# Index scores in pairs of heads between the v tiles, and the k and q norms two tiles at a time with ScalarE multiplying

## The chip, the cores and the metric

The kernel runs on one core of one Trainium2 chip. The metric is the device time of one execution in microseconds. The core has TensorE (matrix products, 1.2 or 2.4 GHz as granted), VectorE, ScalarE and GpSimd, each with its own instruction queue, and SyncE, whose queue here issues most of the DMAs. The queues meet only at semaphores.

## The reference, cut to what matters

One step of a hybrid decoder layer for a prompt of 1024 rows and eight sample rows with 8192 cached keys each. One input projection of the normalised rows gives q, k, v, two gates, the index queries qi, one index key ki, the index weights wi and the inputs of a convolution.

```python
q = _rms_norm(zq.reshape(B, T, N_HEADS, HEAD_DIM), q_g)
k = _rms_norm(zk.reshape(B, T, N_KV_HEADS, HEAD_DIM), k_g)
...
# _index_select: for each query the 256 keys of the highest score
s = jnp.einsum('thd,ld->thl', qi, ki).astype(jnp.float32) * (IDX_DIM ** -0.5)
score = jnp.einsum('th,thl->tl', wi.astype(jnp.float32) * (N_IDX_HEADS ** -0.5), jax.nn.relu(s))
score = jnp.where(k_pos[None, :] <= q_pos[:, None], score, -jnp.inf)
_, idx = lax.top_k(score, k_sel)
```

Eight heads of 64 values, 8 index heads of 64, all in float32. The chosen keys are attended (the kernel masks the others), the convolution branch (31 taps a channel, layer norm, silu) runs beside it, both are gated, projected by w_out and added to x.

## The kernel before, in words

The order on every engine is written out by hand; PsumPlan hands out the eight PSUM banks b0 to b7 and makes each new user of a bank wait until the one before has been read. A projection whose rows lie on partitions is done in nine tiles (`natural(g, t)`, t = 8 the eight sample rows: eight products of 512 columns), one whose channels lie there in twelve pieces (`transposed(g, m)`: eight products of 344 columns). In the trace every float32 product is two MATMUL rows.

The stages of TensorE are: x transposed; kw (index keys and weights); glub and glua in pieces; qi in pieces; the index stage; v in tiles, ga and gc in pieces, beside the search; k and q in tiles with their norms and transpositions; the attention of the prompt by blocks of 128 queries, from the last block to the first, with the samples' attention in between; the output projection.

VectorE works through `taps`: 4 channel groups of 31 multiply-adds over 1024 columns (ctmp, L1267). Ahead of the last twelve of them it prepares Qb and Wb, the samples' index queries and weights, and the samples' own score (`sn`, L1294 to L1298). TensorE's `own_score()` (one small product of sn and selnew) stands behind the tenth of the twelve qi pieces and waits for it.

In the index stage, blocks i = 2 to 7 of queries have eight heads each over (i + 1) x 128 keys (blocks 0 and 1 keep all their keys). Per head ScalarE copies the queries into one half of qz, whose other half is zero (L1043); TensorE multiplies the whole height of 128 by kiT into a pair of banks, SA or SB; ScalarE takes the relu (L1058), and VectorE adds it with its weight into SC (L1310, L1313). Every five heads a turn of the cached keys comes between, eight in all: GpSimd gathers index keys into cin, VectorE transposes four tiles to ct (L1241), TensorE multiplies by Qb (`cached(n)`), ScalarE takes the relu to drelu, TensorE weighs it (`weigh`, drelu and Wb), ScalarE writes sc16a or sc16b, SyncE's DMAs bring it by way of memory to SD.

The search finds the 256th highest score of each row bit by bit in 32 rounds. VectorE writes candidates (candn, L1373) and counts three of the seven groups of rows, ScalarE the other four (sgj, L1088); between its rounds ScalarE evacuates v, ga and gc from PSUM, about one tile or piece a round. At its end stand the exact threshold and a scan (dC, L1406). Only then do the norms begin.

The norm stage goes through NORMED: k tiles 0 to 7, k of the samples, q tiles 7 to 0, q of the samples, numbered n = 0 to 17. TensorE computes tile n and transposes tile n - 3 (`norm_transpose`). ScalarE squares tile n to nsq (L1133) and copies the transposed tile to kT or qT. VectorE's `norm(n)` sums the squares of each head (L1482), takes the reciprocal root in a chain of twelve short instructions that each wait for the one before, multiplies the tile by it (L1493) and by the gain (L1497). zN has two places. Between the norms VectorE has masks for the six searched blocks (n = 2 to 7), positions of the chosen cached keys (n = 2 to 5, with TensorE's rank rows at n = 5 to 8), pages and addresses (n = 6, 7), the bias of those keys (n = 8, eight times L1469 and a sum) and the centring of the convolution (n = 9). ScalarE squares the centred halves (lnsq) and TensorE sums them in `row_variances`.

## Time and profile before

| | |
|---|---|
| median of 3 runs | 1040.39 us (1034.81 to 1040.89) |
| the profiled execution | 1040.58 us |
| its span from first to last instruction | 1038.8 us |
| mean granted clock of TensorE | 0.946 of 2.4 GHz |
| busy: TensorE, VectorE, ScalarE, GpSimd | 930.8, 694.0, 372.5, 85.4 us |
| chain that ended last: TensorE, VectorE, ScalarE | 72%, 21%, 3% of the span |

The times of the views are microseconds from the first instruction of the span. A busy share says how much an engine worked, not whether the end hung on it: that is to be read stage by stage, from what each engine waited for.

### The profile page before, as it was taken

Reading aid. Unit: us, or ns where it says so; the run is one execution under the profiler, and the core shown is the slowest. Engines: PE = TensorE matmul, PEld = TensorE weight load, DVE = VectorE, ACT = ScalarE, POOL = GpSimd, SP = SyncE. Lnnn points to the kernel's source line nnn. Section 1 sums busy time; section 2 is a strip of 40 time slices with the busy share of each in tenths; the row PEclk is TensorE's granted clock in tenths of the full one; section 3 lists DMA queues with packets and bytes.
Section 4 is the critical chain, followed back from the end, with each engine's and each line's share of the span. In section 5 each row is a group of like instructions: output and inputs, shape, how many; then the busy total and the mean of one; then the engine's idle time right before and its main releaser. Section 6 shows DMA issues by size and latency. Waiting matters only on the chain.

```text
span 1038.8 us, 11317 instructions
## 1 busy us (share of the span) xinstructions
PE 930.8 (90%) x3900; PEld 514.4 (50%) x3900; DVE 694.0 (67%) x1598; ACT 372.5 (36%) x830; POOL 85.4 (8%) x90
## 2 busy tenths in 40 slices
PE   3999999936899999999998899697598789999998
PEld 2866666713243444666643334353366555445432
DVE  5309987999896765888878889966487565432111
ACT  6310101102666656889700000122765364221000
POOL 0211010000541000000000000001011101310000
PEclk9999999877999999999999899788699789999999
DMA  8363020200662302001030000005012102320211
GB/s 291 108 188 62 1 81 3 83 0 1 203 210 83 112 34 84 26 22 61 0 102 21 21 20 12 0 1 210 21 52 61 31 11 62 104 100 31 71 62 42
DMA packets 35314, 69.82 MB, mean 67 GB/s; under 512 B 9609, under 2 KB 11953, under 8 KB 35249
## 3 DMA queue, kind: packets, MB, share of 16 engines
q1 hardware_dynamic: 28089, 43.93, 13.0%
q0 software_dynamic: 7168, 25.17, 7.4%
q8 instruction: 31, 0.51, 0.2%
q14 instruction: 26, 0.21, 0.1%
HBM read 58.46 MB, written 11.11 MB: 67 GB/s over the span
## 4 chain that ended last, share of the span: by engine, by line
PE 72%; DVE 21%; ACT 3%; issue 3%; DMA 1%; SPq 1%; DVEq 0%; ACTq 0%
PE ps L491 67%; DVE ctmp L1267 8%; PE ps L494 4%; DVE ct L1241 1%; DMA xn<-in_x_prompt 1%; DVE pv L1469 1%; ACT PTs L942 1%; ACT uT L1120 1%; DVE LB L1470 1%; DVE mcum L1395 0%; DVE zN L1493 0%; ACT relu L1058 0%; DVE pv L1435 0%; DVE uT L1675 0%; ACT sqj L955 0%
## 5 line engine op out<-in xcount | busy, mean ns | idle before, releaser
L491 PE MATMUL ps<-xT,W 128*128 128x344 f32 x960 | 283.8, 458 | 0.0
L491 PEld LDWEIGHTS ps<-xT,W 128*128 128x128 f32 x960 | 184.0, 193 | 97.6 <-issue 5.6
L491 PE MATMUL ps<-W,xT 128*128 128x512 f32 (+3 forms) x576 | 214.7, 531 | 1.2 <-ACT relu L1058 1.2
L1267 DVE SCALAR_TENSOR_TENSOR ctmp<-uT,chw,ctmp 128x1024 f32<-128x1024 f32 x116 | 152.0, 1310 | 4.1
L491 PEld LDWEIGHTS ps<-W,xT 128*128 128x128 f32 (+1 forms) x576 | 94.9, 185 | 113.7 <-issue 113.3
L1088 ACT ACTIVATE sgj<-SC,candn 128x1024 bf16<-128x1024 f32 (+3 forms) x128 | 114.5, 897 | 8.8 <-DVE candn L1373 6.6
L942 ACT ACTIVATE PTs<-ps 128x512 f32<-128x512 f32 (+3 forms) x96 | 43.1, 484 | 125.7 <-PE ps L494 125.7
L1706 DVE TENSOR_TENSOR ps<-ps,TP 128x256 f32<-128x256 f32 (+1 forms) x64 | 26.4, 412 | 71.2 <-PE ps L491 70.8
L1133 ACT ACTIVATE nsq<-ps 128x512 f32<-128x512 f32 (+1 forms) x18 | 10.7, 596 | 164.5 <-DVE nss L1482 120.9
L491 PE MATMUL ps<-kiT,qz 128*128 128x512 f32 (+3 forms) x160 | 61.7, 530 | 7.6 <-ACT relu L1058 6.5
L494 PE MATMUL ps<-Cc,Pm 128*128 128x128 f32 x288 | 46.6, 303 | 17.7 <-ACT PTs L942 17.5
L491 PE MATMUL ps<-W,uT 128*128 128x512 f32 x128 | 60.1, 612 | 0.0
L491 PE MATMUL ps<-W,qT 128*128 128x512 f32 x128 | 58.7, 600 | 0.0
L1711 DVE CUSTOM_DVE_ANT_0 Pm<-ps,SC 128x1024 f32<-128x1024 f32 (+7 forms) x64 | 48.5, 758 | 9.7 <-PE ps L494 7.7
L1785 POOL DMA_INDIRECT KVr<-in_cache_k,idx x16 | 16.0, 999 | 472.9 <-DVE zq L1497 369.8
L494 PEld LDWEIGHTS ps<-Cc,Pm 128*128 128x128 f32 x288 | 34.5, 153 | 40.1 <-issue 38.2
L1147 ACT ACTIVATE Pm<-Pm,mn 128x1024 f32<-128x1024 f32 (+7 forms) x64 | 49.5, 774 | 11.8 <-DVE mn L1711 11.2
L1686 DVE TENSOR_TENSOR resid<-resid,ps 128x512 f32<-128x512 f32 (+1 forms) x18 | 12.3, 684 | 60.8 <-PE ps L491 60.8
L1752 POOL DMA_INDIRECT cin<-in_cache_k_idx,pidx x32 | 36.8, 1149 | 170.3 <-DVE ct L1241 134.4
L491 PE MATMUL ps<-kT,qT 64*128 64x512 f32 (+3 forms) x192 | 44.6, 572 | 6.1 <-DVE mn L1711 3.6
L491 PEld LDWEIGHTS ps<-kiT,qz 128*128 128x128 f32 x160 | 27.8, 189 | 42.8 <-issue 39.0
L1313 DVE SCALAR_TENSOR_TENSOR SC<-relu,wI,SC 128x384 f32<-128x384 f32 (+5 forms) x42 | 39.7, 946 | 8.2 <-ACT relu L1058 6.1
(308 smaller groups left out, 1046.4 us busy)
## 6 DMA issues: line engine op xcount, KB each, us to landing
W<-in_w_in SPq DMA_DIRECT2D x8, 2048.0 KB, 8.7
xn<-in_x_prompt SPq DMA_DIRECT2D x8, 512.0 KB, 8.2
W<-in_w_out SPq DMA_DIRECT2D x1, 4096.0 KB, 13.3
resid<-in_x_prompt SPq DMA_DIRECT2D x16, 256.0 KB
out<-resid SPq DMA_DIRECT2D x16, 256.0 KB
out<-V SPq DMA_DIRECT2D x8, 256.0 KB
out<-zN SPq DMA_DIRECT2D x8, 256.0 KB, 2.0
bias_rows<-tprow SPq DMA_DIRECT2D x1, 1536.0 KB
```

Source lines behind the costliest of these rows:

```text
L491: return nc.tensor.matmul(out, lhsT, rhs, start=start, stop=stop)
L494: return nc.tensor.transpose(out, in_, ident[0:n, 0:n])
L942: nc.scalar.activation(out, in_, func, scale=scale).then_inc(plan.drain_sem(tag), 1)
L1088: last = nc.scalar.activation(sgj[:, j, 0:s.shape[1]], s, ACT.Sign, bias=candn[:, j:j + 1].bitcast(F32), accum_out=acnt[:, j:j + 1])
L1147: nc.scalar.activation(Pm[:, n % 3, 0:L], Pm[:, n % 3, 0:L], ACT.Exp, bias=mn[:, n % 4:n % 4 + 1], scale=-1.0, accum_out=sums[:, n:n + 1]) ...
L1267: ins = vec.scalar_tensor_tensor(conv[:, c, :] if j == CW - 1 else acc_, src, chw[:, c, j:j + 1], acc_, ALU.mult, ALU.add)
L1313: vec.scalar_tensor_tensor(sc(i), relu[:, n % 2, 0:L], wI[:, i, h:h + 1], sc(i), ALU.mult, ALU.add).then_inc(relu_used, 1)
L1686: vec.tensor_tensor(resid[u % 2][0:r, :], resid[u % 2][0:r, :], pt(("y", u))[0:r, :], ALU.add).then_inc(plan.drain_sem(("y", u)), 1)
L1706: link(vec.tensor_tensor(s[:, L - bw:L], s[:, L - bw:L], TP[:, h, BAND - bw:BAND], ALU.subtract))
L1711: vec.tensor_tensor_reduce(out=Pm[:, n % 3, 0:L], in0=s, in1=m, scale=1.0, scalar=3.0e38, op0=ALU.add, op1=ALU.min, accum_out=mn[:, n % 4: ...
L1752: pool.indirect_dma_start(out=cin[:, ch % 4, :], out_offset=None, in_=pages_ap, in_offset=bass.IndirectOffsetOnAxis(ap=pidx[:, ch % 8, ch ...
L1785: pool.indirect_dma_start(out=dst, out_offset=None, in_=src.rearrange("a n k h d -> (a n k) (h d)"), in_offset=bass.IndirectOffsetOnAxis(a ...
```

## The change

There are two edits. The first concerns the index stage. qz goes: a chunk is now a block, a pair of heads and at most 512 keys (CHUNKS, 40 of them), and TensorE multiplies the two heads from the two halves of qiT's height by the two halves of kiT's into two banks (b2 and b3, or b4 and b5). The chunks are spread over the slots of the v tiles: in each slot half of them stand in the middle of a v tile, and the others behind it (`halves`), the last block's eight in the ninth slot. v uses only b0 and b1. Relu has four places of 512 columns, where TP lies later, so that TP is loaded after the last weighting. sc16b lies in SC's last block, so that block waits until its DMAs are out (scd_out). ScalarE evacuates all nine v tiles in these slots, and the search starts with ga. VectorE does all its taps ahead of Qb, Wb and the own score, and TensorE's own_score() stands behind the second v tile. `cached_turn` 1 to 7 stand one to a slot, `cached` 0 to 5 likewise, and 6 and 7 together in slot 7.

The second edit concerns the norms. VectorE's chain runs for two tiles at once, at odd n; ScalarE multiplies (`scaled`, eight activations a tile, each with its own scale); VectorE multiplies by the gain only for k and the sample's q (`gained`), while q's gain goes into the scale with which qT is copied (qgc, loaded and scaled at the start). Transpositions and copies stand one tile later, and so do or two tiles later the other pieces between the norms; rank rows on TensorE stay.

```diff
-    relu = sb("relu", [P, 2, 1024], F32, rV)
-    sc16 = [sb("sc16a", [16, 32, 2, 16], F32, rKV), sb("sc16b", [16, 32, 2, 16], F32, rV + 8192)]
+    relu = sb("relu", [P, 4, 512], F32, rTP)
+    sc16 = [sb("sc16a", [16, 32, 2, 16], F32, rKV), sb("sc16b", [16, 32, 2, 16], F32, rSC + 12800)]
...
-    INDEX_STEPS = [(i, h) for i in range(2, NT) for h in range(H)]
+    CHUNKS = [(i, hp, a) for i in range(2, NT) for hp in range(H // 2) for a in range(0, (i + 1) * P, 512)]
+    def width(n):
+        i, hp, a = CHUNKS[n]
+        return min(512, (i + 1) * P - a)
+    FIRST_SLOT, SLOTS = 2, NT + 1
+    def chunks_in(s):
+        last = sum(1 for x in CHUNKS if x[0] < NT - 1)
+        if s == SLOTS - 1:
+            return range(last, len(CHUNKS))
+        k, n = s - FIRST_SLOT, SLOTS - 1 - FIRST_SLOT
+        return range(max(k, 0) * last // n, max(k + 1, 0) * last // n)
+    def cached_in(s):
+        return [6, 7] if s == 7 else [s - 1] if 1 <= s < 7 else []
+    def halves(s):
+        c = chunks_in(s)
+        return c[:len(c) // 2], c[len(c) // 2:]
+    EVACUATED_EARLY = NT + 1
...
-        def natural(g, t):
+        def natural(g, t, banks=4, between=None):
...
-            o = begin(("z", g, t), f"b{ring[0] % 4}")
+            o = begin(("z", g, t), f"b{ring[0] % banks}")
             ring[0] += 1
             for k in range(KC):
+                if between and k == KC // 2:
+                    between()
...
-                last.then_inc(ct_used, 1)
-            nc.tensor.matmul(ps[0:1, 6, 0:1], ident[0:1, 0:1], ident[0:1, 0:1], start=True, stop=True) \
-                .then_inc(plan.fill_sem(("ds", n)), 1)
+                last.then_inc(ct_used if g < 3 else plan.fill_sem(("ds", n)), 1)
...
-        done = 0
-        for n, (i, h) in enumerate(INDEX_STEPS):
-            wait(qz_ready, n + 1)
-            begin(("ix", i, h), ("SA", "SB")[n % 2])
-            L = (i + 1) * P
-            o = pair_of(("ix", i, h), L)
-            for a in range(0, L, 512):
-                b = min(a + 512, L)
-                last = mm(o[:, a:b], qz[:, h % 2, n // 2 % 2, :], kiT[:, a:b])
-            last.then_inc(plan.fill_sem(("ix", i, h)), 1)
-            while done < cached_before(n):
-                cached(done)
-                done += 1
-        for t in range(NT + 1):
-            natural("v", t)
+        def index_scores(n):
+            i, hp, a = CHUNKS[n]
+            for m in range(PIECES):
+                wait(*plan.drained(("zt", "qi", m)))
+            for t in range(i + 1):
+                wait(*plan.drained(("kt", t)))
+            for e in range(2):
+                begin(("ix", n, e), f"b{2 + 2 * (n % 2) + e}")
+            for e in range(2):
+                r = slice(64 * e, 64 * e + 64)
+                mm(pt(("ix", n, e))[:, 0:width(n)], qiT[r, hp, i * P:(i + 1) * P], kiT[r, a:a + width(n)]).then_inc(plan.fill_sem(("ix", n, e)), 1)
+        for s in range(SLOTS):
+            one, two = halves(s)
+            def between():
+                for n in one:
+                    index_scores(n)
+            natural("v", s, 2, between)
+            for n in two:
+                index_scores(n)
+            if s == 1:
+                own_score()
+            for n in cached_in(s):
+                cached(n)
...
-            wait(zn_ready, n + 1)
+            wait(zn_ready if g == "k" else z_scaled, n + 1)
...
-            if n >= 3:
-                norm_transpose(n - 3)
+            if n >= 4:
+                norm_transpose(n - 4)
...
+        def index_relu(n):
+            for e in range(2):
+                tag = ("ix", n, e)
+                u = 2 * n + e
+                act.wait_ge(*plan.full(tag))
+                if u >= 4:
+                    act.wait_ge(relu_used, u - 3)
+                nc.scalar.activation(relu[:, u % 4, 0:width(n)], pt(tag)[:, 0:width(n)], ACT.Relu, scale=HD ** -0.5).then_inc(plan.drain_sem(tag), 1)
...
+        for s in range(SLOTS):
+            for n in chunks_in(s):
+                index_relu(n)
+            for n in cached_in(s):
+                cached_out(n)
+            evacuate("v", s)
+        ev = EVACUATED_EARLY
...
-                     scale=1.0 if g == "k" else -HD ** -0.5)
+                     scale=1.0 if g == "k" else qgc[:, 0:1])
+        def scaled(n):
+            g, t = NORMED[n]
+            r = P if t < NT else NB
+            act.wait_ge(norms_ready, n // 2 + 1)
+            if n >= 2:
+                g2, t2 = NORMED[n - 2]
+                if t2 < NT:
+                    act.wait_ge(*plan.full(("tr", g2, t2)))
+                if g2 == "k":
+                    act.wait_ge(zn_out[n % 2], zn_stored(n - 2))
+            for h in range(H):
+                hs = slice(h * HD, (h + 1) * HD)
+                last = nc.scalar.activation(zN[0:r, n % 2, hs], pt(("z", g, t))[0:r, hs], ACT.Copy, scale=nrs[0:r, n % 2 * 8 + h:n % 2 * 8 + h + 1])
+            last.then_inc(plan.drain_sem(("z", g, t)), 1)
+            act.wait_ge(*plan.drained(("z", g, t)))
+            nc.scalar.activation(ss[0:NB, 15:16], ss[0:NB, 14:15], ACT.Copy).then_inc(z_scaled, 1)
...
-            if n >= 3:
-                norm_out(n - 3)
-            if n == 10:
+            if n >= 2 and n % 2 == 0:
+                scaled(n - 2)
+                scaled(n - 1)
+            if n >= 4:
+                norm_out(n - 4)
...
-        taps(CW + 24, NTAP - 12)
+        taps(CW + 24, NTAP)
...
+        def weighted(n):
+            i, hp, a = CHUNKS[n]
+            if (i, hp, a) == (NT - 1, 0, 0):
+                v.wait_ge(scd_out[1], 128)
+            for e in range(2):
+                u, h = 2 * n + e, 2 * hp + e
+                src, dst = relu[:, u % 4, 0:width(n)], sc(i)[:, a:a + width(n)]
+                v.wait_ge(*plan.drained(("ix", n, e)))
+                if h == 0:
+                    vec.tensor_scalar(dst, src, wI[:, i, 0:1], None, ALU.mult).then_inc(relu_used, 1)
+                else:
+                    v.wait_ge(relu_used, u)
+                    vec.scalar_tensor_tensor(dst, src, wI[:, i, h:h + 1], dst, ALU.mult, ALU.add).then_inc(relu_used, 1)
+        for s in range(SLOTS):
+            for n in chunks_in(s):
+                weighted(n)
+            if 1 <= s < 8:
+                cached_turn(s)
...
-            z = pt(("z", g, t))[0:r, :].rearrange("p (h d) -> p h d", h=H)
+            c = n % 2 * 8
             v.wait_ge(nsq_done, n + 1)
-            vec.reduce_sum(nss[0:r, :], nsq[0:r, :].rearrange("p (h d) -> p h d", h=H), AXX).then_inc(nsq_used, 1)
-            v.wait_ge(nsq_used, n + 1)
-            link(vec.tensor_scalar(nss[0:r, :], nss[0:r, :], 1.0 / HD, EPS, ALU.mult, ALU.add))
-            rsqrt(nrs[0:r, :], nss[0:r, :], ntm[0:r, :])
+            vec.reduce_sum(nss[0:r, c:c + 8], nsq[0:r, :].rearrange("p (h d) -> p h d", h=H), AXX).then_inc(nsq_used, 1)
+            if n % 2:
+                v.wait_ge(nsq_used, n + 1)
+                if n >= 3:
+                    v.wait_ge(z_scaled, n - 1)
+                link(vec.tensor_scalar(nss[:], nss[:], 1.0 / HD, EPS, ALU.mult, ALU.add))
+                rsqrt(nrs[:], nss[:], ntm[:])
+                vec.memset(dsc[:, 7:8], 0.0).then_inc(norms_ready, 1)
+        def gained(n):
+            g, t = NORMED[n]
+            if (g, t) != ("q", NT) and g == "q":
+                return
+            r = P if t < NT else NB
             o = zN[0:r, n % 2, :].rearrange("p (h d) -> p h d", h=H)
-            if n >= 2:
-                g2, t2 = NORMED[n - 2]
-                if t2 < NT:
-                    v.wait_ge(*plan.full(("tr", g2, t2)))
-                if g2 == "k":
-                    v.wait_ge(zn_out[n % 2], zn_stored(n - 2))
-            vec.tensor_tensor(o, z, nrs[0:r, :].unsqueeze(2).broadcast_to([r, H, HD]), ALU.mult).then_inc(plan.drain_sem(("z", g, t)), 1)
-            v.wait_ge(*plan.drained(("z", g, t)))
+            v.wait_ge(z_scaled, n + 1)
...
+            if n >= 3:
+                gained(n - 3)
...
+        for half in range(2):
+            sp.dma_start(qgc[64 * half:64 * half + 64, :], qg[0:1, :].rearrange("a d -> d a"), allow_slow_non_contiguous=True).then_inc(q_gain_in, 16)
...
+        sp.wait_ge(relu_used, 2 * len(CHUNKS))
+        sp.wait_ge(tp_out, 16)
+        sp.dma_start(TP[:], bass.AP(tpd.tensor, P - 1, [[FW - 1, P], [P * FW, H], [1, BAND]])).then_inc(tp_in, 16)
```

On TensorE, between the last qi pieces and the second cached turn, before (kiT with qz are the index scores, ct with Qb a cached turn, drelu with Wb its weighing):

```order
L491 MATMUL ps<-xT,W 128x344 x24
L491 MATMUL ps<-sn,selnew 128x1
L491 MATMUL ps<-xT,W 128x344 x16
L491 MATMUL ps<-kiT,qz 128x384 x5
L491 MATMUL ps<-ct,Qb 32x512 x8
L638 MATMUL ps<-Cc 1x1
L491 MATMUL ps<-kiT,qz 128x384 x3
L491 MATMUL ps<-kiT,qz 128x512 x2
```

and of the changed kernel (W with xT are eight or four products of a v tile, kiT with qiT the pairs):

```order
L516 MATMUL ps<-xT,W 128x344 x40
L516 MATMUL ps<-W,xT 128x512 x16
L516 MATMUL ps<-sn,selnew 128x1
L516 MATMUL ps<-ct,Qb 32x512 x8
L516 MATMUL ps<-W,xT 128x512 x4
L516 MATMUL ps<-kiT,qiT 128x384 x4
L516 MATMUL ps<-W,xT 128x512 x4
L516 MATMUL ps<-kiT,qiT 128x384 x4
L516 MATMUL ps<-kiT,qiT 128x512 x2
L516 MATMUL ps<-ct,Qb 32x512 x8
L516 MATMUL ps<-drelu,Wb 16x512
```

The own score moved behind the two qi pieces and two v tiles, the first cached turn right behind it, and each later v tile is cut in two by chunks.

On VectorE, from the third group of taps to the first index scores, before:

```order
L1267 SCALAR_TENSOR_TENSOR ctmp<-uT,chw,ctmp 128x1024 x18
L1280 COPY Qb<-ps 32x8x8 x4
L1286 MEMSET dsc 128x1
L1288 TENSOR_TENSOR Wb<-ps,Cc 128x4x4x4
L1294 TENSOR_TENSOR zN<-srow,kiS 8x512
...
L1298 TENSOR_REDUCE sn<-sn 8x1
L1300 TENSOR_TENSOR SD<-ps,Cc 128x1
L1267 SCALAR_TENSOR_TENSOR ctmp<-uT,chw,ctmp 128x1024 x11
L1267 SCALAR_TENSOR_TENSOR uT<-uT,chw,ctmp 128x1024
L1310 TENSOR_SCALAR SC<-relu,wI 128x384
L1313 SCALAR_TENSOR_TENSOR SC<-relu,wI,SC 128x384 x4
```

and of the changed kernel:

```order
L1317 SCALAR_TENSOR_TENSOR ctmp<-uT,chw,ctmp 128x1024 x29
L1317 SCALAR_TENSOR_TENSOR uT<-uT,chw,ctmp 128x1024
L1330 COPY Qb<-ps 32x8x8 x4
L1336 MEMSET dsc 128x1
L1338 TENSOR_TENSOR Wb<-ps,Cc 128x4x4x4
L1344 TENSOR_TENSOR zN<-srow,kiS 8x512
...
L1348 TENSOR_REDUCE sn<-sn 8x1
L1350 TENSOR_TENSOR SD<-ps,Cc 128x1
L1291 STREAM_TRANSPOSE ct<-cin 128x1024 x4
L1362 TENSOR_SCALAR SC<-relu,wI 128x384
L1365 SCALAR_TENSOR_TENSOR SC<-relu,wI,SC 128x384 x7
```

The last twelve taps stand ahead of Qb, Wb and sn, and a turn of transpositions ahead of the first weighting.

On ScalarE at the start of the norms, before (nsq are squares, kT the copy of a transposed tile):

```order
L1133 ACTIVATE nsq<-ps 128x512 x4
L942 ACTIVATE kT<-ps 128x4x128
L1133 ACTIVATE nsq<-ps 128x512
L942 ACTIVATE kT<-ps 128x4x128
L1133 ACTIVATE nsq<-ps 128x512
L942 ACTIVATE kT<-ps 128x4x128
L1133 ACTIVATE nsq<-ps 128x512
```

and of the changed kernel (zN from ps and nrs are the eight multiplications of a tile, ss the short copy behind which z_scaled is raised):

```order
L1174 ACTIVATE nsq<-ps 128x512 x3
L1147 ACTIVATE zN<-ps,nrs 128x64 x8
L1150 ACTIVATE ss<-ss 8x1
L1147 ACTIVATE zN<-ps,nrs 128x64 x8
L1150 ACTIVATE ss<-ss 8x1
L1174 ACTIVATE nsq<-ps 128x512 x2
L1147 ACTIVATE zN<-ps,nrs 128x64 x8
L1150 ACTIVATE ss<-ss 8x1
L1147 ACTIVATE zN<-ps,nrs 128x64 x8
L1150 ACTIVATE ss<-ss 8x1
L975 ACTIVATE kT<-ps 128x4x128
L1174 ACTIVATE nsq<-ps 128x512
```

Two tiles are multiplied at each even n, ahead of the copies, and the squares of the next tile stand behind the second of them.

## Rows read from the trace of the kernel before

**Rows 1.** Two stretches: busy time of each engine, clock, DMA share, GB/s

```profile
253.00:346.00 93.00, 84.77 (x320) 33.09 (x320) 76.59 (x78) 60.72 (x119) 30.56 (x31) 1.00 0.51 164
547.00:716.00 169.00, 148.01 (x453) 68.21 (x451) 137.81 (x389) 23.11 (x41) 0.00 (x0) 0.91 0.06 20
```

**Rows 2.** Timeline of TensorE, 239 to 520 us (start, duration, operation, count, idle before)

```profile
239.72 0.58 PE L491 MATMUL ps<-sn,selnew 8*128 8x1 f32 x2 [23.96 <-DVE sn L1298]
240.23 11.77 PE L491 MATMUL ps<-xT,W 128*128 128x344 f32 x32
258.09 1.94 PE L491 MATMUL ps<-ct,Qb 128*32 128x512 f32 x16
268.97 1.03 PE L491 MATMUL ps<-drelu,Wb 128*16 128x512 f32 x2
331.19 14.00 PE L491 MATMUL ps<-kiT,qz 128*128 128x512 f32 x32
346.40 62.13 PE L491 MATMUL ps<-W,xT 128*128 128x512 f32 x144 [1.21 <-ACT relu L1058]
408.46 111.31 PE L491 MATMUL ps<-xT,W 128*128 128x344 f32 x384
```

**Rows 3.** TensorE in the attention stage: pairs of 1024 and 512 columns

```profile
750.86 1.99 PE L491 MATMUL ps<-kT,qT 64*128 64x512 f32 x8
871.13 1.13 PE L491 MATMUL ps<-kT,qT 64*128 64x512 f32 x4
```

**Rows 4.** Timeline of VectorE: last taps, weightings, transpositions

```profile
240.41 14.49 DVE L1267 SCALAR_TENSOR_TENSOR ctmp<-uT,chw,ctmp 128x1024 f32<-128x1024 f32 x11
256.66 2.79 DVE L1313 SCALAR_TENSOR_TENSOR SC<-relu,wI,SC 128x384 f32<-128x384 f32 x4
260.11 4.62 DVE L1241 STREAM_TRANSPOSE ct<-cin 128x1024 f32<-128x1024 f32 x4 [0.66 <-PE ps L491]
346.29 1.28 DVE L1313 SCALAR_TENSOR_TENSOR SC<-relu,wI,SC 128x1024 f32<-128x1024 f32 x1 [0.43 <-ACT relu L1058]
```

**Rows 5.** VectorE in the search: candidates 1, 12 and 31, and dC

```profile
352.87 0.17 DVE L1373 TENSOR_SCALAR candn<-thr 128x4 uint32<-128x4 uint32 x1
423.64 0.17 DVE L1373 TENSOR_SCALAR candn<-thr 128x4 uint32<-128x4 uint32 x1
510.77 0.17 DVE L1373 TENSOR_SCALAR candn<-thr 128x4 uint32<-128x4 uint32 x1
533.96 1.23 DVE L1406 TENSOR_TENSOR_SCAN dC<-dE 128x513 f32<-128x513 f32 x1
```

**Rows 6.** Groups of ScalarE by form: count, busy us, mean ns, idle before

```profile
L1043 ACT ACTIVATE qz<-qiT 64x128 f32<-64x128 f32 x48 | 14.7, 307 | 1.2
L970 ACT ACTIVATE kiN<-ps 128x128 f32<-128x128 f32 x8 | 2.2, 278 | 11.2 <-PE ps L491 11.2
```

**Rows 7.** VectorE's norm of one tile, and the group of key bias products

```profile
550.30 0.66 DVE L1482 TENSOR_REDUCE nss<-nsq 128x8 f32<-128x512 f32 x1
553.41 0.69 DVE L1493 TENSOR_TENSOR zN<-ps,nrs 128x512 f32<-128x512 f32 x1
...
L1469 DVE TENSOR_TENSOR pv<-ohb,rbB 128x512 f32<-128x512 f32 x8 | 8.7, 1084 | 0.2
```

**Rows 8.** TensorE in the norm stage, and its first scores

```profile
550.68 8.81 PE L491 MATMUL ps<-W,xT 128*128 128x512 f32 x16
661.38 1.12 PE L494 MATMUL ps<-Cc,zN 128*128 128x128 f32 x4 [10.21 <-DVE zN L1497]
716.32 3.42 PE L491 MATMUL ps<-kT,qT 64*128 64x512 f32 x8 [2.49 <-DVE zN L1493]
```

**Rows 9.** SyncE's queue, and the landing times of the loads of W

```profile
331.96 2.62 SPq L1871 DMA_DIRECT2D decode_scores<-sc16b  x4
336.76 0.35 SPq L1874 DMA_DIRECT2D SD<-decode_scores  x1
...
DMA to landing us min/median/max: 8.0/8.9/12.0
```

116 lines of the change are left out of this document (42 added, 74 removed).

## The prediction

> **What bounds the kernel now.** I read the timeline of TensorE first, then that of VectorE for the stretches in which TensorE waits, then the table of windows. From 31 us on TensorE works almost without a gap; only four places matter here. (1) After ten of the twelve pieces of qi it waits 23.96 us for the sample's own index score, which VectorE reaches late among its taps [rows 2]. (2) From 253 to 346 us, the index stage, TensorE is busy 84.8 us of 93 and VectorE 76.6 us: the two hand each head to each other [rows 1]. (3) The search on VectorE and ScalarE runs from 348.2 to 535.2 us, and TensorE covers it with v (62.1 us), ga and gc and four k tiles; TensorE gets to the end of them only at 547 us, so in this stretch it is the bound [rows 2, 5]. (4) From 547 to 716 us come the k and q norms: TensorE busy 148.0 us of 169 and VectorE 137.8, with one wait of 10.21 us for VectorE and short ones besides [rows 1, 8]. What follows 716.32 us (322.5 us) holds the same instructions afterwards, and I carry it over unchanged.
>
> **Taps to own score.** The last 12 taps move ahead of the own score. At 1.32 us each (14.49/11, [rows 4]) they are 15.8 us, so the score, ready at 239.7 us before, is ready at 255.5. All of VectorE's work up to 256.2 us is the same work in another order, so VectorE starts on index scores when it did. TensorE gets two qi pieces at 4.64 us (111.31/24 for such pieces, [rows 2]) and two v tiles at 6.9 us ahead of the wait, which began at 215.8 us: 215.8 + 9.3 + 13.8 = 238.9 us, and then 16.6 us of wait instead of 24. So of the nine v tiles only two lie beside the taps: own_score stands behind the second one, and everything behind it waits. The idle time drops the granted clock; the two pieces after the old wait took 11.77 us instead of 9.3 [rows 2], so I charge 2.5 us for the way back to full clock, as before.
>
> **Index stage.** Seven v tiles, 40 chunks and eight turns of cached scores now stand in a row on TensorE. Prices: v tile 62.13/9 = 6.9 us; a cached turn 1.9 + 1.0 us for its weighing [rows 2]. A pair of heads on half the rows each: 1.99 us for 1024 columns and 1.13 us for 512 [rows 3], against 1.75 us for one head of 1024 before (14.00/8, [rows 2]). That is 1.67 ns a column for both heads, plus 0.2 us where the shape changes. All 40 chunks: 16,896 columns, 28.2 us, and 14 to 40 changes, 3 to 8 us: 31 to 36.5 us, I take 34 (26 of it ahead of the last eight chunks). It was 61.7 before, so pairing saves 28 us of TensorE. From 256.0 us: cached turn 1.9, six tiles 41.4, chunks 26, seven turns 13.3, eight weighings 7.7, clock 2.5 = 92.8 us, to 348.8. The seventh and eighth turn stand back to back, and the eighth needs four transposes (4.62 us, [rows 4]) that VectorE starts only when the seventh frees the tiles: 4 to 5 us of wait, to 353.
> VectorE is not the bound until then: a weighting costs 0.70 us at 384 columns and 1.32 at 1024 start to start [rows 4], so 0.33 us plus 0.97 ns a column; cutting at 512 adds 32 instructions, 10 us. Its sum is 43 us for the first 32 chunks and 32 for the transposes, 75 of 97 us; its slack sits in the half tiles of v that it waits for. The last eight chunks (block 7, all 512 wide) turn it round: 16 weightings at 0.82 = 13.1 us. They may start when the last decode scores have left sc16b. Before, their four DMAs began to be issued at 331.96 us and the DMA that waits for their landing at 336.76 [rows 9]: 4.8 us, so at 358.5; TensorE interposes half a tile (3.45 us) once, which costs about 1 us. VectorE ends at 373.1 instead of 347.6: **the stage costs 25.5 us more**. Bounds: 18 us if pairs and handovers are at their cheap end, 36 if each handover of a chunk shows as it did in the old stage, where VectorE idled 16 of 93 us [rows 1].
> W for ga is issued behind the scores' DMAs, at about 359 us, and needs 8.0 to 12.0 us to land [rows 9]: 367 to 371 us, and TensorE wants it at 368 to 369. Up to 2 us, in the slack ahead of the first evacuation. TP's load moves behind it; it is needed at 715 us and costs nothing. The two small loads of qgc put at most some 3 us before the page indices near 30 us, hidden since the gathered pages are first wanted at 48.5 us.
>
> **Search.** Rounds paced by v took 6.87 us; rounds with a piece or nothing take (510.77 - 423.64)/19 = 4.586 us [rows 5]. From the first candidate to the last it was 157.9 us for 30 rounds; now 30 x 4.586 + 0.7 for one table load = 138.3: **19.6 us less**. The head of it (4.7 us) and the 24.4 us from the last candidate to dC stay [rows 5]. The search starts at 373.8 (0.7 us for the mask on POOL) and dC stands at 541.2 instead of 535.2. TensorE runs out of work at about 508 us (111 us of ga and gc, 28 us of four k tiles) and idles 33 us: cover that v gave and that the search no longer needs.
>
> **Norms.** VectorE per tile now: a sum 0.7, and per two tiles one chain of 12 short steps (553.41 - 550.30 less the sum of 0.7: 2.4 us, [rows 7]). It loses 9 chains (22 us), 18 multiplications (0.72, 13 us) and the gain of eight q tiles (6 us): 41 us. ScalarE takes over eight activations of 64 columns a tile. The nearest rows: 128 columns from PSUM 278 ns, of which the next one overlaps 0.1 us, and from SBUF 307 ns [rows 6]. I take 8 x 0.13 + 0.1 + 0.2 for the closing copy = 1.4 us, bounds 1.0 and 2.7.
> The Trainium skill, "VectorE: DVE Perf Modes", section on the TRN2 errata, speaks against such narrow instructions: each pays its fixed part, 172 cycles on ScalarE from PSUM. As an estimate from that page eight of them are 1.6 us, which would add about 0.5 us at each of three handovers; the overlapping starts of rows 6 speak for less.
> Followed, with dC as zero (before in brackets): k4 starts at 8.8 (15.5), since the fifth tile needs only the first multiplied one; but the first transposition waits for VectorE behind a mask, and the rank rows are through at 35 (36). The key bias block (eight products of 1.1 and eight sums of 0.7 us, 14.6 us with the gaps, [rows 7]) moves two tiles on, beside q5, the two means and q4, so the 10.21 us wait [rows 8] goes: q4 starts at 101.5 (109). Three waits take its place. ScalarE in its order multiplies tile n-1 only when the transposition of n-3 has run, one tile later on TensorE, and the squares for the row variances stand behind that: 3.7 and 4.2 us. A new wait stands in each chain too: nrs is there once, so VectorE may overwrite it only when the pair before is multiplied; masks, position rows and with them TensorE's rank rows are queued behind. By hand it is met in time, at the closest by 1 us. At the end the last two tiles go one after the other through squares, chain, multiplication and copy: 6 us. Slow tiles behind waits and narrow products (8.81 against 6.9 us, [rows 8]) I counted as often as before. The scores start at 174.2 instead of 181.1: **6.9 us less**.
>
> **Sum.** 25.5 - 19.6 - 6.9 = -1.0. The profiled execution took 1040.58 us, 1.8 more than its span of 1038.8, and the median of the three is 1040.39. Forecast: 1040 us, no change. About 1% is what a measurement of this kernel can tell from none.
>
> **Rivals.** *The norms run at TensorE's own pace (faster).* TensorE's busy time from 547 to 716 is 148 us [rows 1]. If ScalarE is never late, the 14 us of the three waits go: 1026 us. For it: ScalarE is idle most of this stretch. Against: its order is fixed and has the later transposition in it. Chance 0.22.
> *The norms in twos hold TensorE (slower).* If VectorE, behind masks and position rows, finishes a chain late, or waits there for the pair before, the tile four further on finds no free bank, and TensorE waits once per pair: 2 us in seven pairs, 14 us: 1054 us. It decides where a pair's chain comes after two tile times (14 us). For it: VectorE is busy 137.8 of 169 us there today [rows 1]; against: 41 us leave it. Chance 0.2.
> *The edit doesn't do what it says:* the pairs do not overlap among full-height tiles, and TensorE pays up to 28 us in the stage that it bounds: 1066 us. Against it: the pairs of the attention stage do [rows 3]. Chance 0.08.
>
> **How the numbers follow.** Forecast 0.5. The range holds it, the first rival and the second with 3 us at the upper end for the index bounds: 1025 to 1057; outside are the third and the tails. Faster by over 1% 0.25, within 0.47, slower 0.28.
>
> **What would show it.** Wait before the own score about 17 us; last weighting near 373; candidates 4.6 us apart from the first; TensorE idle some 33 us before the end of the search; scores' start near 715. I am wrong if TensorE isn't busy through the v tiles after 256 us, if the rounds aren't short at once, or if the norm stage takes other than 165 to 185 us from dC to the scores.

## The result, and the profile after

The changed kernel takes 1064.56 us (median of 4, 1063.41 to 1067.55) against 1039.84 us before (median of 4): ratio 1.025, 95% interval 1.022 to 1.028. It is slower by 25 us. The forecast of 1040 us was wrong, and the range of 1025 to 1057 us did not hold the time. The profiled execution took 1065.68 us with a span of 1063.9 us, its mean granted clock of TensorE was 0.919 (0.946 before). Three of the twelve executions of one kernel below, the index edit alone, and single ones of five others took 12 us or more longer at a lower clock; the medians below leave these out, so that 1041.8 us stands where some expectations say 1042.7.

Four marks divide both traces; the difference of the last column is what the forecast has to answer for.

| | before | after | difference | forecast |
|---|---|---|---|---|
| search starts | 348.2 | 379.9 | +31.7 | +25.5 |
| search start to dC | 187.0 | 167.2 | -19.8 | -19.6 |
| dC to first scores | 181.1 | 192.6 | +11.5 | -6.9 |
| first scores to end of span | 322.5 | 324.2 | +1.7 | 0 |

The marks of after, first VectorE's, then TensorE's (timeline: start, duration, line, operation, count, idle before and what ended it):

```profile
379.91 0.06 DVE L1418 MEMSET candn<- 128x4 uint32 x1 [0.46 <-POOL SC L1841]
...
545.92 1.23 DVE L1459 TENSOR_TENSOR_SCAN dC<-dE 128x513 f32<-128x513 f32 x1
```

```profile
256.32 0.58 PE L516 MATMUL ps<-sn,selnew 8*128 8x1 f32 x2 [18.23 <-DVE sn L1348]
257.20 3.67 PE L516 MATMUL ps<-ct,Qb 128*32 128x512 f32 x16 [0.30 <-issue]
...
547.20 0.59 PE L516 MATMUL ps<-dC,Cc 128*128 128x1 f32 x2 [32.93 <-DVE dC L1459]
...
669.74 0.60 PE L519 MATMUL ps<-Cc,zN 128*128 128x128 f32 x4
674.55 6.99 PE L516 MATMUL ps<-Cc,lnsq 128*128 128x1 f32 x32 [4.21 <-ACT lnsq L1155]
681.39 10.15 PE L516 MATMUL ps<-W,xT 128*128 128x512 f32 x16
...
704.07 6.54 PE L516 MATMUL ps<-Cc,lnsq 128*128 128x1 f32 x32 [4.77 <-ACT lnsq L1155]
710.46 9.28 PE L516 MATMUL ps<-W,xT 128*128 128x512 f32 x16
...
738.72 1.09 PE L519 MATMUL ps<-Cc,zN 128*128 128x128 f32 x4 [6.53 <-ACT qT L975]
739.73 1.23 PE L516 MATMUL ps<-kT,qT 64*128 64x512 f32 x2
```

The reader is to see three things. The wait for the own score is 18.2 us where it was 24.0 [rows 2]. TensorE now idles 32.9 us ahead of dC, where before it came to dC 12 us late. And the tiles behind the row variances that had to wait are slow: 10.15 and 9.28 us, while an undisturbed one takes 7.0.

The table of windows of after (length, busy time of TensorE, of its loads, VectorE, ScalarE, POOL, granted clock), to be laid beside [rows 1]; the last line is the norm stage:

```profile
257.00:359.30 102.30, 95.27 (x368) 34.49 (x369) 70.69 (x93) 40.28 (x93) 27.96 (x31) 0.98 0.39 126
380.00:547.00 167.00, 134.28 (x434) 82.03 (x432) 147.88 (x571) 127.53 (x289) 0.00 (x0) 0.91 0.13 45
547.00:740.00 193.00, 159.87 (x454) 76.77 (x456) 108.59 (x281) 56.02 (x204) 0.00 (x0) 0.84 0.13 48
```

VectorE is relieved (108.6 us of 193, against 137.8 of 169 in [rows 1]; from dC to the scores its busy time fell from 142.2 to 108.4 us, by 34 where the forecast, which counts the gaps within its chains too, had 41), and it buys nothing: the clock fell from 0.91 to 0.84 and TensorE waits 33 us in all.

### The profile page after: what moved, and what is told of

It is laid out like the page before. It is cut to its first block, busy times and chain, and to the rows that moved or that the text cites. A ratio compares the mean times of both kernels' runs of the same rounds, so it can differ in the third digit from the quotient of the medians.

```text
span 1063.9 us, 11407 instructions
## 1 busy us (share of the span) xinstructions
PE 920.2 (86%) x3884; PEld 508.4 (48%) x3884; DVE 667.1 (63%) x1506; ACT 389.5 (37%) x976; POOL 82.3 (8%) x89
## 4 chain that ended last, share of the span: by engine, by line
PE 58%; DVE 21%; ACT 16%; issue 3%; DMA 1%; SPq 0%; DVEq 0%; ACTq 0%; POOL 0%; POOLq 0%
PE ps L516 54%; ACT sgj L1110 11%; DVE ctmp L1317 8%; PE ps L519 4%; DVE SC L1365 1%; ACT zN L1147 1%; DMA xn<-in_x_prompt 1%; ACT PTs L975 1%; DVE eqm L1386 1%; ACT uT L1161 1%; DVE mcum L1448 1%; DVE thr L1430 1%; DVE tk L1429 1%; DVE candn L1426 1%; DVE cnt L1404 1%
## 5 line engine op out<-in xcount | busy, mean ns | idle before, releaser
L516 PE MATMUL ps<-xT,W 128*128 128x344 f32 x960 | 280.8, 455 | 0.3 <-ACT relu L1079 0.3
L516 PE MATMUL ps<-W,xT 128*128 128x512 f32 (+3 forms) x576 | 221.9, 541 | 4.4 <-ACT zN L1147 4.4
L516 PEld LDWEIGHTS ps<-W,xT 128*128 128x128 f32 (+1 forms) x576 | 95.7, 188 | 123.2 <-issue 118.1
L1365 DVE SCALAR_TENSOR_TENSOR SC<-relu,wI,SC 128x512 f32<-128x512 f32 (+3 forms) x70 | 46.2, 660 | 25.1 <-ACT relu L1079 18.8
L1079 ACT ACTIVATE relu<-ps 128x512 f32<-128x512 f32 (+3 forms) x80 | 36.2, 526 | 51.7 <-PE ps L516 51.5
L1147 ACT ACTIVATE zN<-ps,nrs 128x64 f32<-128x64 f32 (+1 forms) x144 | 31.2, 322 | 55.9 <-PE ps L519 32.3
L1813 POOL DMA_INDIRECT cin<-in_cache_k_idx,pidx x32 | 33.1, 1034 | 198.8 <-DVE ct L1291 161.8
```

Of the source, the lines that this page charges most:

```text
L516: return nc.tensor.matmul(out, lhsT, rhs, start=start, stop=stop)
L1079: nc.scalar.activation(relu[:, u % 4, 0:width(n)], pt(tag)[:, 0:width(n)], ACT.Relu, scale=HD ** -0.5).then_inc(plan.drain_sem(tag), 1)
L1147: last = nc.scalar.activation(zN[0:r, n % 2, hs], pt(("z", g, t))[0:r, hs], ACT.Copy, scale=nrs[0:r, n % 2 * 8 + h:n % 2 * 8 + h + 1])
L1365: vec.scalar_tensor_tensor(dst, src, wI[:, i, h:h + 1], dst, ALU.mult, ALU.add).then_inc(relu_used, 1)
L1813: pool.indirect_dma_start(out=cin[:, ch % 4, :], out_offset=None, in_=pages_ap, in_offset=bass.IndirectOffsetOnAxis(ap=pidx[:, ch % 8, ch ...
```

## The experiments

All kernels are built on one of two: the changed kernel, or the index edit alone. Each was timed in five rounds beside the kernel before; times are medians, ratios are against the kernel before. Stages are read from one traced execution of each kernel, which need not be the median one. The start of the index stage drifts by some 2 us between kernels with the same code up to there (the own score at 255.1 to 257.5 us), so a stage's end is read from the own score.

**The two edits apart.** The first takes every line of the diff that belongs to the v tiles and the index scores, the second every line of the norms. In the norm stage the two differ in this:

```
-                norm_transpose(n - 3)
+                norm_transpose(n - 4)
...
+            if n >= 2 and n % 2 == 0:
+                scaled(n - 2)
+                scaled(n - 1)
```

> The index edit alone, with the norms of the kernel before. If the two edits act each in its own stage and do not touch each other, this takes the 31.7 us that the index stage lost and the 19.8 us that the search gave back, and keeps the norm stage of before at 181 us from dC to the first scores: about 1052 us (1050 to 1055). If the norm stage is slow in the changed kernel because of what the index edit did ahead of it (33 us in which TensorE idles before dC, where before it idled 23), the norm stage takes about 190 us here too and the kernel about 1062 us.

> The norms edit alone, with the index stage of the kernel before. If the norms in twos are themselves what costs, dC to the first scores takes 190 to 194 us instead of 181 and the kernel 1050 to 1053 us. If the cost came from the index edit ahead of it, this is at or below 1040 us, down to 1033 us if the forecast of 174 us for the norm stage holds.

Index edit alone: 1041.8 us, ratio 1.002 (1.000 to 1.005). Norms alone: 1062.6 us, 1.022 (1.019 to 1.025). So the norms edit carries 22 us of the 25. The index edit came out 10 us below the 1052 us expected, nearly all of it the head start told below. It is no matter of what stands ahead of it: dC to the scores took 171.9 us in the first (545.8 to 717.7), 20.7 less than in the changed kernel, and 201.9 us in the second (537.3 to 739.2), 20.8 more than before (this trace, of 1068.3 us, is the slowest of the six executions). The expectation for the norms alone was too low (190 to 194 us): the comparison with before had hidden that the index edit by itself makes this stage 9.2 us shorter (171.9 against 181.1), because TensorE stands ready at dC with its four k tiles done and not 12 us behind it. Windows of the norm stage, index edit alone, then norms alone:

```profile
546.00:718.00 172.00, 149.57 (x454) 69.92 (x456) 142.50 (x405) 24.21 (x43) 0.00 (x0) 0.89 0.10 37
```

```profile
537.00:739.00 202.00, 170.11 (x481) 81.61 (x479) 108.83 (x281) 56.04 (x203) 0.00 (x0) 0.87 0.12 45
```

Between the first and the changed kernel TensorE runs the same 454 instructions. It is idle 22.4 us in the one and 33.1 us in the other, and busy 149.6 against 159.9: half of the 20.7 us are waits, half are slower products.

**The clock, by products that nobody reads.** In the changed kernel:

```
+        def fill(count, bank):
+            for _ in range(count):
+                mm(ps[:, bank, :], xT[:, 0, 0:P], xT[:, 0, 0:512])
...
+            fill(36, 7)
             wait(made["equals_counted"], 1)
```

> The changed kernel with products that nobody reads (xT times xT, 512 columns) put on TensorE where it waited: 36 ahead of the first use of dC, 4 and 5 behind that, 4 and 5 ahead of the two row variances, 7 ahead of the last but one transposition. They are meant to end just before the wait does. Theory: the norm stage loses to the granted clock, which was 0.84 of full speed in it, and tiles of 7.0 us took 8.7 to 10.2 us right behind the waits; with the gaps filled the clock stays up, the tiles take 7.0 us, and dC to the scores falls by 10 to 14 us to 179 to 183 us, the kernel to 1050 to 1055 us. Rival: the waits on ScalarE and the coupling by twos are the cost, and the clock only a sign of them: then nothing is gained, 1064 to 1067 us.

1056.4 us, ratio 1.015 (1.012 to 1.018): 8.2 us less, of which 6.2 between dC and the scores (186.4 us) and 3.0 behind them. The clock up to dC was 1.00 instead of 0.91, and the first tile behind dC took 7.03 us instead of 9.46. The time lies between what the theory (1050 to 1055 us) and its rival (1064 to 1067 us) expected. The tiles that cost most stayed slow:

```profile
668.90 3.60 PE L516 MATMUL ps<-xT 128*128 128x512 f32 x8
673.27 5.67 PE L516 MATMUL ps<-Cc,lnsq 128*128 128x1 f32 x32 [0.78 <-ACT lnsq L1171]
678.80 10.18 PE L516 MATMUL ps<-W,xT 128*128 128x512 f32 x16
...
701.51 3.73 PE L516 MATMUL ps<-Cc,lnsq 128*128 128x1 f32 x32 [0.49 <-ACT lnsq L1171]
705.10 8.81 PE L516 MATMUL ps<-W,xT 128*128 128x512 f32 x16
```

The tile behind the row variances took 10.18 and 8.81 us with no long wait ahead. So a slow tile needs no long wait ahead of it: in the index edit alone the tile behind the second row variances (32 products of one column, with no wait) takes 8.81 us too. The clock is part of the loss, and the 10 to 14 us expected of it were too many.

**The squares ahead of the scaling.** ScalarE's order in the changed kernel, two lines moved:

```
+            if n == 12:
+                squares(0, half_of(0), lnsq)
...
             if n >= 2 and n % 2 == 0:
                 scaled(n - 2)
                 scaled(n - 1)
...
-            if n == 12:
-                squares(0, half_of(0), lnsq)
```

> The changed kernel with ScalarE squaring the centred halves ahead of the two tiles that it scales, where it now does it behind them. Both waits of TensorE ahead of its row variances (4.2 and 4.8 us) should go. If the waits themselves are the cost, 9 us less: 1055 us. If the clock is, each wait removed also spares the slow tile behind it (3.1 and 2.3 us): 1050 us. If the products then wait for the scaled tiles instead (their banks come free 3 us later), 1062 to 1065 us.

1051.8 us, ratio 1.011 (1.008 to 1.013), 12.8 us less, near the 1050 us expected if each wait also costs a slow tile; dC to the scores 179.4 us. Of the two waits one is left with 1.9 us:

```profile
670.41 6.66 PE L516 MATMUL ps<-Cc,lnsq 128*128 128x1 f32 x32 [1.91 <-ACT lnsq L1155]
676.93 9.15 PE L516 MATMUL ps<-W,xT 128*128 128x512 f32 x16
...
693.66 3.63 PE L516 MATMUL ps<-Cc,lnsq 128*128 128x1 f32 x32
697.15 8.81 PE L516 MATMUL ps<-W,xT 128*128 128x512 f32 x16
```

7.1 us of waiting went, and with it 4.7 us in the products behind: the second row variances run in 3.63 us instead of 6.54, the other three in 6.66, 9.15 and 8.81 instead of 6.99, 10.15 and 9.28. This one order is over half of what the norms edit lost.

**The tail too.** On top of the run before, separate columns of nss, nrs and ntm for alternate pairs, and ScalarE takes the square of the last tile ahead of `scaled(15)`.

```
-                if n >= 3:
-                    v.wait_ge(z_scaled, n - 1)
+                if n >= 5:
+                    v.wait_ge(z_scaled, n - 3)
...
+            if n == 17:
+                scaled(15)
+                norm_out(12)
+                norm_out(13)
```

> The changed kernel with the squares first, as in the run before it that took 1051.8 us, and with its tail mended: two sets of columns for the norms, so that the last pair's reciprocal roots start without waiting for the pair before, the square of the last tile ahead of the fifteenth tile's scaling. If the 8 us that TensorE waits in the tail are the chain of ScalarE and VectorE work behind the last tile, 3 to 5 us go: 1047 to 1049 us, and the norms in twos then cost 4 to 6 us against the index edit alone at 1042.7 us. If the chain only shifts to another wait, 1051 to 1052 us.

1051.6 us, ratio 1.010 (1.007 to 1.014): level with the run before, where 1047 to 1049 us had been hoped for. The scores start earlier (175.8 us behind dC), but take longer, 327.6 us against 324.7. TensorE's waits between dC and the scores are now 23.0 us in all, as good as the 22.4 of the index edit alone. The first 40 us of the scores in three kernels, index edit alone, the changed one, this one:

```profile
717.70:757.70 40.00, 26.37 (x156) 15.43 (x156) 26.39 (x37) 26.50 (x40) 5.04 (x6) 0.83 0.29 110
```

```profile
739.70:779.70 40.00, 26.93 (x123) 15.19 (x124) 22.61 (x34) 26.35 (x38) 5.02 (x5) 0.71 0.12 35
```

```profile
721.60:761.60 40.00, 27.39 (x109) 15.29 (x108) 21.03 (x32) 24.78 (x36) 5.02 (x5) 0.59 0.19 69
```

The clocks of 0.83, 0.71 and 0.59 go with 320.8, 324.2 and 327.6 us from the first scores to the end. The same work is done more slowly: 4.9 of the 6.8 us between the first and the last of the three lie in the first 54 us. That the handovers of the tail are the reason is not shown. The kernel before has the same tail as the index edit alone, and its first 40 us run at 0.71.

**Scaling on ScalarE without the twos.** The changed kernel, with each tile's norm by itself and the squares at n = 10 and 13 as before; position rows, pages and key biases stand one tile later than before.

```
-            if n >= 2 and n % 2 == 0:
-                scaled(n - 2)
-                scaled(n - 1)
-            if n >= 4:
-                norm_out(n - 4)
+            if n >= 1:
+                scaled(n - 1)
+            if n >= 3:
+                norm_out(n - 3)
```

> The changed kernel with ScalarE still multiplying and the gains of q still in the transposition's copy, but each tile's norm by itself again, transposed three tiles later and not four, the row variances' squares where they were before. This parts the two halves of the norms edit. If the twos cost the 20.7 us (each tile waits for its partner, ScalarE's two scaled tiles in a row stand ahead of the squares), it takes 1038 to 1043 us, like the index edit alone. If ScalarE's scaling in eight pieces is the cost, even one at a time, 1050 to 1060 us.

1052.0 us, ratio 1.014 (1.011 to 1.017), within what the second theory expected, which put the cost on ScalarE's scaling even one tile at a time. From dC to the scores it takes 181.8 us, 9.9 more than with the norms of before and 10.8 less than the changed kernel, so the first theory keeps a part. The first transposition now waits 10.0 us where two waits of 4.7 and 1.8 stood, since a k tile passes from VectorE to ScalarE and back to VectorE for its gain; the transposition ahead of the row variances waits for ScalarE:

```profile
559.06 1.12 PE L519 MATMUL ps<-Cc,zN 128*128 128x128 f32 x4 [10.01 <-DVE zN L1552]
...
680.97 1.11 PE L519 MATMUL ps<-Cc,zN 128*128 128x128 f32 x4 [6.61 <-ACT ss L1150]
```

So the scaling on ScalarE costs some 10 us in this form. The other 10.8 us can't be put down to the pairing as such: with the twos kept and only the squares first, the stage took 179.4 us, 2.4 less than with the tiles one at a time. What the twos cost in the changed kernel is above all the place of the squares behind two scaled tiles.

**Filling in two more kernels.** First the kernel with both repairs, filled like the first but not ahead of the row variances (36, 4, 5, and 5 ahead of the last transposition but one); then the index edit alone, filled with 36, 5, 2 and 10:

```
+            if n == 3:
+                fill(5, 7)
+            if n == 12:
+                wait(*plan.drained(("tr",) + NORMED[6]))
+                fill(10, 4)
             if n >= 3:
                 norm_transpose(n - 3)
```

> The changed kernel with both repairs of its norm stage (1051.6 us), and filling products: 36 ahead of the first use of dC, 4 and 5 behind it, 5 ahead of the last transposition but one. The first 40 us of the scores, which ran at a granted clock of 0.50 and 0.65 behind the waits of the tail (0.80 and 0.84 with the norms of before), should run at 0.8, worth 4 to 6 us there, and the first tile behind dC at full clock, worth 2 us: 1043 to 1047 us. If the low clock in the scores has another reason than the waits ahead of them, 1049 to 1051 us.

> The index edit alone, norms of before, with products that nobody reads where TensorE waits: 36 ahead of the first use of dC (it waits 32.9 us there), 5 and 2 between the first normed tile and the second use of dC (4.7 and 1.8 us), 10 ahead of the tenth tile's transposition (9.1 us). Three tiles behind those waits took 9.6, 8.8 and 9.1 us where others took 7.0. If the clock is what they lose, 5 to 7 us go: 1036 to 1038 us against 1042.7 us without them. If the filling ends too late or the clock is lost elsewhere as before (the rank rows, the row variances), 1041 to 1044 us.

The repaired one fell from 1051.6 to 1043.4 us, 1.006 (1.003 to 1.008). All of that lies behind the first scores (318.2 us instead of 327.6); dC to the scores stayed at 175.2. The time is the one expected, the way to it only in part: of the 9.4 us only 3.4 lie in the first 54 us of the scores, whose first 40 us ran at 0.74 and not 0.8, and why the rest went is open. The index edit alone rose from 1041.8 to 1051.0 us, 1.009 (1.006 to 1.013), against both theories. Up to the two means it keeps pace (95.6 us behind dC, 95.0 without filling); then, in the filled kernel and in the one without:

```profile
656.23 8.75 PE L511 MATMUL ps<-xT 128*128 128x512 f32 x20
666.66 0.66 PE L514 MATMUL ps<-Cc,zN 128*128 128x128 f32 x4 [1.68 <-DVE zN L1532]
...
675.78 0.66 PE L514 MATMUL ps<-Cc,zN 128*128 128x128 f32 x4 [1.59 <-DVE zN L1532]
676.27 6.33 PE L511 MATMUL ps<-Cc,lnsq 128*128 128x1 f32 x32
682.46 9.39 PE L511 MATMUL ps<-W,xT 128*128 128x512 f32 x16
```

```profile
663.85 1.12 PE L514 MATMUL ps<-Cc,zN 128*128 128x128 f32 x4 [9.11 <-DVE zN L1519]
664.76 9.05 PE L511 MATMUL ps<-W,xT 128*128 128x512 f32 x16
673.65 0.60 PE L514 MATMUL ps<-Cc,zN 128*128 128x128 f32 x4
674.09 3.63 PE L511 MATMUL ps<-Cc,lnsq 128*128 128x1 f32 x32
677.58 7.11 PE L511 MATMUL ps<-W,xT 128*128 128x512 f32 x16
```

Filling the 9.1 us wait moved the low clock from one tile (9.05 us) to the row variances and the next tile (6.33 and 9.39 instead of 3.63 and 7.11), and the scores behind it run slower (325.6 us against 320.8). Its single times lie between 1040 and 1052.5 us, wider than without filling (1040 to 1047 us), so where the low stretch falls may also change from one execution to the next; a single trace can't show that. Why it falls where it does is open; that a filled wait always pays is refuted.

**The key biases spread.** Index edit alone, three, three and two heads in three tiles, the centring and the first half's squares one tile later.

```
-            if n == 8:
-                for h in range(H):
+            if 8 <= n <= 10:
+                for h in range(3 * (n - 8), min(3 * (n - 7), H)):
                     key_bias(h)
-            if n == 9:
+            if n == 10:
                 center(0, 0, half_of(conv, 0), 512)
```

> The index edit alone, norms of before, with the eight key biases (14.7 us of VectorE work in one piece, behind which TensorE waits 9.1 us for a normed tile and then runs at low clock) spread over three tiles, and the centring one tile later. If that piece is what TensorE waits for, the wait and the slow tile behind it go, 5 to 10 us: 1033 to 1038 us. If VectorE is simply full there (busy from 605 us to 672 us without a break), the wait comes back in pieces: 1041 to 1043 us.

1046.1 us, ratio 1.007 (1.004 to 1.010): slower by 4.3 us than without, and outside both expectations. The wait of 9.1 us shrank to 2.7, but the squares came later, and TensorE waited 7.45 us for them at the row variances, with 6.98 us for those. As in the changed kernel, squares that come late are paid for at the row variances.

**What holds the end of the index stage.** Index edit alone, `sc16b` in the taps' region instead of the last block's; then the last block's chunks spread over all slots and the eighth cached turn in the last slot:

```
-sb("sc16b", [16, 32, 2, 16], F32, rSC + 12800)
+sb("sc16b", [16, 32, 2, 16], F32, rGC)
...
-        last = sum(1 for x in CHUNKS if x[0] < NT - 1)
-        if s == SLOTS - 1:
-            return range(last, len(CHUNKS))
-        k, n = s - FIRST_SLOT, SLOTS - 1 - FIRST_SLOT
+        last = len(CHUNKS)
+        k, n = s - FIRST_SLOT, SLOTS - FIRST_SLOT
```

> The index edit alone, with the second buffer of the cached scores in a place of its own, so that VectorE no longer waits 10.6 us for its transfer ahead of the last block; the last block's chunks stay in the last slot. Theory: TensorE sets the end of the index stage and brings the last block's products no earlier than 361.5 us, so VectorE gets at most 1 us: 1041.5 to 1043 us. Rival: the transfer was what held the stage, and 5 to 8 us go: 1035 to 1038 us.

> As the run before, and the last block's chunks spread over all seven slots instead of the last one, with the eighth cached turn in the last slot instead of behind the seventh. TensorE's work is the same, but its three waits around the last two turns (1.8 and 1.5 us, and some 2 us of low clock) are covered and VectorE no longer runs 4 us behind TensorE at the end. Theory: 5 to 9 us less in the index stage, 1034 to 1038 us. Rival: the decode scores, whose transfer to SD takes 10 us from the last turn, now end the stage, and what is gained is 0 to 3 us: 1040 to 1043 us.

1041.5 us, 1.002 (0.999 to 1.004), as the theory said, and 1045.0 us, 1.004 (1.001 to 1.006), slower than theory and rival. From the own score to the search: 123.2 us for the index edit alone, 123.6, and 120.9. The wait for the transfer turned into one for the products, as the theory had it:

```profile
365.29 0.49 DVE L1331 TENSOR_SCALAR SC<-relu,wI 128x512 f32<-128x512 f32 x1 [9.62 <-ACT relu L1076]
```

The spreading gained 2.3 us there against the index edit alone, within the rival's 0 to 3, and the search took 170.5 instead of 167.2 us. TensorE stood without weights at its start:

```profile
376.42 8.94 PE L509 MATMUL ps<-xT,W 128*128 128x344 f32 x22 [3.98 <-DMA W<-in_w_in]
```

**The load earlier, and v tiles back into the search.** `load_w(5)` ahead of the cached scores' transfers in SyncE's queue; then with three, then five of the nine v tiles behind the stage:

```
         load_w(4)
+        load_w(5)
         for n in range(1, 8, 2):
...
+        for t in range(EVACUATED_EARLY, NT + 1):
+            natural("v", t)
         for m in range(PIECES):
             transposed("ga", m)
```

> The index edit alone with the last block's chunks spread over the slots (1045.0 us), and the load of ga's weights issued ahead of the cached scores' transfers instead of behind them. There the search began 2.2 us earlier but took 170.5 us instead of 167.2, while TensorE waited 4.0 us for those weights at its start. If the late weights are why the search took longer, the 3.3 us come back: 1040 to 1042 us. If not, 1044 to 1046 us.

> As the run before, and the last three v tiles (21 us of TensorE) behind the index stage, in the search, where TensorE idled 33 us ahead of dC. Theory: TensorE's work sets the index stage, so its end comes 10 to 20 us earlier until VectorE sets it, and the search, with 21 us of TensorE work more and 12 us of idling left, takes 0 to 5 us longer: 1025 to 1035 us. Rival: VectorE and ScalarE are nearly as full there and the search pays for the tiles' copies as before, 1038 to 1043 us.

> The same with five v tiles in the search (35 us of TensorE against 33 us of idling). If TensorE's work is what binds both stages, this is level with three tiles or up to 3 us faster; if VectorE binds the index stage by then, the search alone grows, and it is 2 to 8 us slower than with three.

| kernel | us | ratio | own score to search | search | dC to scores |
|---|---|---|---|---|---|
| before | 1040.4 | | 108.5 | 187.0 | 181.1 |
| index edit alone | 1041.8 | 1.002 | 123.2 | 167.2 | 171.9 |
| chunks spread | 1045.0 | 1.004 | 120.9 | 170.5 | 173.0 |
| and W early | 1037.7 | 0.999 (0.997 to 1.001) | 119.9 | 167.2 | 171.9 |
| and three v tiles late | 1031.9 | 0.992 (0.989 to 0.995) | 108.4 | 170.0 | 173.7 |
| and five v tiles late | 1032.1 | 0.993 (0.990 to 0.995) | 103.2 | 174.7 | 173.4 |

(In the kernel before, 12 taps, 15.8 us, stand behind the own score; in the others ahead of it.) The late load was the 3.3 us of the search (W early came out below the 1040 to 1042 us expected, three tiles late as the theory said, and five level with three). The medians differ by 7.3 us, more than that, because the kernel with the chunks spread ran in two groups, five times at 1040 to 1041.5 us, the traced one among them (1041.1), and six times at 1045 to 1049, and the one with W early nine times of eleven at 1036 to 1038.5; what makes the groups is not shown. Three tiles (21 us of TensorE) taken from the stage shorten it by 11.5 us and lengthen the search by 2.8; two more (14 us) give 5.2 and take 4.7. So TensorE's work did set a good part of the stage, and with five tiles less it waits there for ScalarE's relu:

```profile
334.30 3.40 PE L509 MATMUL ps<-kiT,qiT 64*128 64x512 f32 x8 [4.00 <-ACT relu L1082]
```

TensorE's idling ahead of dC went from 32.5 us to 15.6 with three and 6.4 with five tiles late. Both kernels beat the one before by 8 us, and the changed one by 32; all of that is without the norms edit.

## Why the prediction was wrong

*The step that failed* stands in the part on the norms: "Slow tiles behind waits and narrow products ... I counted as often as before", and the sum on it, 174.2 us from dC to the scores, measured 192.6. The waits themselves were nearly right. Forecast 3.7 and 4.2 us at the row variances and 6 at the end, measured 4.2, 4.8 and 6.5; k4 at 8.8 us behind dC, measured 9.4; the first rank rows through at 35, measured 35.8. But q4 started at 108.9 us instead of 101.5: k6 and two more tiles behind the rank rows took 9.9, 8.7 and 8.8 us instead of 7.0. From q4 to the scores it took 83.7 us instead of 72.7. Of these 11 us 3 are longer or new waits, and 8 are slow products: each of the two waits at the row variances brought some 3 us more for the row variances (7.0 and 6.5 us for 3.6) and a tile of 9 to 10 us behind, where 8.8 stood before. A wait costs more than its length: 7.1 us of waiting removed gave 13.1 us in the stage, 4.7 of them in slow products. The norm stage missed by 18.4 us, and all the rest by 7.7.

*A second fault hid the first.* The forecast compared the norm stage with the one before in one sum. It contains the head start of 9.2 us which the index edit gives, as the edit alone shows. Take those 9.2 out of the forecast of -6.9, and it amounts to +2.3 us for the norms edit by itself; measured are +20.7. An edit whose own forecast is a loss should have stood as a term of its own.

*The index stage*: +31.7 instead of +25.5. The prices of the chunks held: 1.99 us for 1024 columns, 1.56 us for two chunks of 384. I wrote that TensorE has the last slot at 353 us; it was 359.3. It began the stage 1.2 us later, the halves of the v tiles started 3.63 us apart instead of 3.45 (2 us in twelve), chunks waited for ScalarE's relu for 3.5 us in all, and the first and the last cached turn, at low clock, took 3.6 and some 4 us for 1.9, against 2.5 us charged for low clock. The wait at the last two turns came out at 3.4 us (1.9 and 1.5), forecast 4 to 5. The bound of 36 us held it all. That VectorE's last 16 weightings end the stage was right: 13.1 us forecast, 14.0 measured with a wait of 1.3. Two sums of the prediction are slightly off: its own prices give VectorE 46 us for the first 32 chunks and not 43, and 372.6 us for the end and not 373.1; neither matters to the result.

*The search*: right to 0.2 us, by a first round of 5.11 us, with the table load in it, and 4.59 us from the second on. *TensorE idles 33 us before dC*: 32.9. I named it as cover no longer needed; it was the reserve from which the kernels with late v tiles live.

*ScalarE's scaling*: forecast 1.4 us a tile with the closing copy; measured, eight pieces, the copy, and the next tile:

```profile
554.72 1.75 ACT L1147 ACTIVATE zN<-ps,nrs 128x64 f32<-128x64 f32 x8 [1.99 <-DVE dsc L1542]
556.49 0.20 ACT L1150 ACTIVATE ss<-ss 8x1 f32<-8x1 f32 x1
556.60 1.66 ACT L1147 ACTIVATE zN<-ps,nrs 128x64 f32<-128x64 f32 x8
```

It is 1.88 us from start to start. I had taken the overlap of the 128-column copies for narrow ones; the Trainium skill ("VectorE: DVE Perf Modes", section on the TRN2 errata) charges every narrow instruction its fixed part, an estimate of 1.6 us for the eight, and was nearer to the 1.75 us than my rows.

*The rivals.* "The norms in twos hold TensorE" names the right stage and sign. Its mechanism, a wait once per pair for a free bank, showed only at k4, which waits 4.4 us for the first scaled tile and which the forecast had in its 8.8 us; the other waits that the edit brought are behind ScalarE's order. Its price of 14 us on the sum was too small. The pairs overlap as in the attention stage. What followed the scores I carried over; it took 1.7 us more. Its first 40 us ran at 0.71 in both kernels, so the reason lies elsewhere and stays open. Open, too, is most of what the norms edit still costs when its order is mended, some 10 us (1051.6 us against 1041.8): 3.9 of them lie between dC and the scores, 6.8 behind.

## What to carry to other kernels

When an edit takes work off an engine that is not the last to be waited for, cost what it adds to the handovers: here 34 us less VectorE work bought nothing, and two steps put behind others in ScalarE's order cost over half of a 22 us loss. Cost each of two joined edits against a kernel that has the other one already, so that a head start given by one isn't credited to the other. And where the trace ends a stage with TensorE idle (33 us here), move its work from the stage that it bounds into that gap, and look what else stands ahead of the load which that work needs.
